# Twelve of the 192 expert-weight units loaded in three transfers (112, 8 and 8 rows) instead of one

## The reference

```python
def moe_swiglu(h, w_router, w_gate, w_up, w_down):
    logits = jnp.einsum('td,de->te', xt, w_router, preferred_element_type=jnp.float32)
    top_logit, top_idx = lax.top_k(logits, TOP_K)
    gates = jax.nn.softmax(top_logit, axis=-1)
    ...
        a = xb @ w_gate[e]
        b = xb @ w_up[e]
        y = (jax.nn.silu(a) * b) @ w_down[e]
        return y * gate[:, None].astype(y.dtype)
```

## Time and profile before

| | |
|---|---|
| median of 3 runs | 1385.05 us |
| lowest and highest run | 1382.86 and 1386.51 us |
| the profiled execution, its own time | 1383.68 us |
| its span, first to last instruction | 1381.9 us |
| TensorE busy | 1293.9 us, 94% of the span |
| VectorE, ScalarE, GpSimd busy | 421.2, 278.1, 103.7 us |
| bytes moved by DMA | 443.42 MB |
| largest chain shares | TensorE 83%, DMA 7%, VectorE 5% |

### The profile page before, as it was taken

The page is one execution under the profiler, slowest core; times in us unless marked ns, Lnnn a source line. Parts: engine busy times, 40 slices in busy tenths (PEclk is TensorE's granted clock), DMA queues, the critical chain, the costliest instruction groups (busy, mean ns, idle before and its releaser), DMA issues.

```text
span 1381.9 us, 30957 instructions
## 1 busy us (share of the span) xinstructions
PE 1293.9 (94%) x14359; PEld 803.1 (58%) x14359; DVE 421.2 (30%) x573; ACT 278.1 (20%) x409; POOL 103.7 (8%) x239
## 2 busy tenths in 40 slices
PE   5788999999989886999999999999989999999985
PEld 5776999999978874336344345346334345336333
DVE  5586644444455754011020031030021031031023
ACT  4355444433343533000000000000000000000001
POOL 3231400000000123700000000000000000000000
PEclk9999999999998999999999999999999999999998
DMA  9716755555554057999999999999999999999992
GB/s 312 241 62 215 218 186 185 188 188 187 186 195 148 34 228 320 379 406 389 408 426 424 426 424 424 426 425 425 425 425 426 425 427 422 428 423 424 421 416 97
DMA packets 63734, 443.42 MB, mean 321 GB/s; under 512 B 4440, under 2 KB 6496, under 8 KB 39024
## 3 DMA queue, kind: packets, MB, share of 16 engines
q1 hardware_dynamic: 61456, 433.46, 77.4%
q0 software_dynamic: 2144, 7.90, 2.0%
HBM read 440.30 MB, written 1.05 MB: 319 GB/s over the span
## 4 chain that ended last, share of the span: by engine, by line
PE 83%; DMA 7%; DVE 5%; ACT 1%; SPq 1%; issue 1%; POOL 0%; ACTq 0%; DVEq 0%
PE pd L923 17%; PE pa L914 13%; PE pb L914 13%; PE pc L914 9%; DMA unit<-in_moe_w_down 5%; PE pc L656 3%; PE pc L657 3%; PE pc L658 3%; PE pd L658 2%; PE pd L657 2%; PE pd L656 2%; DMA rwords_b<-in_na_rpb 2%; PE pa L656 2%; PE pa L658 2%; PE pa L657 2%; PE pa L868 2%
## 5 line engine op out<-in xcount | busy, mean ns | idle before, releaser
L923 PE MATMUL pd<-unit,hid 128*32 128x256 f32 x4704 | 260.2, 379 | 9.8 <-DMA unit<-in_moe_w_down 9.8
L914 PE MATMUL pa<-unit,xT 128*32 128x448 f32 x2048 | 240.2, 541 | 3.3 <-DMA unit<-in_moe_w_up 2.1
L914 PE MATMUL pb<-unit,xT 128*32 128x448 f32 x2048 | 240.3, 541 | 0.0
L923 PEld LDWEIGHTS pd<-unit,hid 128*32 128x32 f32 x4704 | 151.2, 110 | 116.4 <-DMA unit<-in_moe_w_down 11.9
L1196 DVE TENSOR_TENSOR w_lo<-ring,w_hi 128x2048 fp32r<-128x2048 f32 x72 | 170.7, 2372 | 139.6 <-ACT w_hi L1012 139.2
L1454 DVE TENSOR_TENSOR hidp<-hid,pa 128x448 f32<-128x448 f32 x16 | 14.8, 924 | 558.4 <-PE pa L914 558.4
L1012 ACT ACTIVATE w_hi<-ring 128x2048 fp32r<-128x2048 f32 x72 | 137.3, 1908 | 69.9 <-PE pb L658 56.4
L914 PE MATMUL pc<-unit,xT 128*32 128x448 f32 x1280 | 149.5, 539 | 0.0
L914 PEld LDWEIGHTS pa<-unit,xT 128*32 128x32 f32 x2048 | 66.3, 110 | 128.1 <-issue 120.4
L914 PEld LDWEIGHTS pb<-unit,xT 128*32 128x32 f32 x2048 | 66.6, 110 | 126.6 <-issue 126.6
L656 PE MATMUL pc<-hT_hi,w_hi 128*128 128x256 f32 x448 | 130.1, 290 | 5.4 <-DVE w_lo L1196 4.0
(11 more groups left out here) (261 smaller groups left out, 1321.9 us busy)
## 6 DMA issues: line engine op xcount, KB each, us to landing
unit<-in_moe_w_gate SPq DMA_DIRECT2D x64, 1792.0 KB, 27.7
unit<-in_moe_w_up SPq DMA_DIRECT2D x64, 1792.0 KB, 26.9
unit<-in_moe_w_down SPq DMA_DIRECT2D x64, 1792.0 KB, 28.8
ring<-in_dense_w_gate SPq DMA_DIRECT2D x8, 2048.0 KB, 8.9
ring<-in_dense_w_up SPq DMA_DIRECT2D x8, 2048.0 KB, 8.9
ring<-in_dense_w_down SPq DMA_DIRECT2D x8, 2048.0 KB, 7.6
ring<-in_w_in SPq DMA_DIRECT2D x7, 2048.0 KB, 7.9
ring<-in_w_out SPq DMA_DIRECT2D x4, 2048.0 KB, 11.7
```

What stands on the lines that cost most here:

```text
L914: ins = mm(bank(half, s)[quad(j)], xT[:, s, dt, :], w[:, at:at + FJ], start=dt == 0, stop=dt == DT - 1)
L923: ins = mm(down_out[s][quad(j)], e[:, half, s, t, :], w, start=half == t == 0 and s != 2, stop=half == 1 and t == FT - 1, skip_group_check ...
```

## The change

One unit in fourteen, from unit 24 on (the units 28, 42, 56, ... 182, twelve in all), is loaded by three transfers: rows 0 to 111, rows 112 to 119, rows 120 to 127. Each adds 16 to the buffer's semaphore, and the counts that TensorE waits for are raised to match. The loads of extra items are single, as before. It is described as loading "one unit in fourteen ... as 112 rows and twice eight rows, so that eight of the sixteen DMA engines carry nine rows of it and eight carry seven".

```diff
+SPLIT_EVERY = 14
+SPLIT_ROWS = (0, 112, 120, P)
...
+        def unit_rows(n):
+
+            return SPLIT_ROWS if n >= UNITS and n % SPLIT_EVERY == 0 else (0, P)
+
+        def loads_of_slot(slot, last):
+
+            return sum(len(unit_rows(n)) - 1 for n in range(slot, last + 1, SLOTS))
+
         def unit_loads(i, u):
             if isinstance(i, int):
-                return (i * UNITS + u) // SLOTS + 1
+                return loads_of_slot(unit_slot(i, u), i * UNITS + u)
             slot = u % EXTRA_SLOTS
-            return (i - NE) * EXTRA_TURNS + (-(-(NE * UNITS - slot) // SLOTS) + u // EXTRA_SLOTS + 1)
+            return (i - NE) * EXTRA_TURNS + (loads_of_slot(slot, NE * UNITS - 1) + u // EXTRA_SLOTS + 1)
...
                 slot = unit_slot(i, u)
-                sp.dma_start(units[slot][:, :], src).then_inc(unit_landed[slot], 16)
+                rows = unit_rows(i * UNITS + u) if isinstance(i, int) else (0, P)
+                for a, b in zip(rows, rows[1:]):
+                    sp.dma_start(units[slot][a:b, :], src[a:b]).then_inc(unit_landed[slot], 16)
```

## The result

| | before | after |
|---|---|---|
| median of the runs | 1383.95 us (4 runs) | 1538.61 us (4 runs) |
| lowest and highest | 1375.71 and 1386.51 | 1537.87 and 1539.76 |
| profiled execution, its span | 1383.68, 1381.9 | 1539.76, 1537.9 |
| TensorE busy | 1293.9 us | 1338.3 us |
| MB on the load queue | 433.46 | 433.47 |

A forecast was written before the change was run, and what follows sets the result against it. The prediction took unit 188's landing, set by the late half of the DMA engines, as the bound. A 5.9 us gain, all other terms 0, took 1385.05 to 1379.2 us; the range was 1377.0 to 1386.5.

The forecast's parts named there:

- What bounds the kernel: End of the kernel: the landing of unit 188, at 1347.1 us, sets the end; all after it is fixed.
- The cadence; about half the engines ahead: Units 42 to 188: 4.382 us each against 4.29, so about half the engines run up to 13.5 us ahead.
- Part 1: Eleven splits in the full queue: a row less on eight late engines lands unit 188 5.9 us earlier.
- rival A: Split units: the nine rows fall on the late eight engines, giving 1391.0 us, +0.43%; chance 0.16.
- Part 2: Other eight engines: 5.9 us more work, 1.7 us still in hand; cost 0, at worst a few tenths.
- Part 3: SP's queue: 24 more issues of 333 ns, 8.0 us in all, hidden by SP's waiting; price 0.
- Part 4: DMA engines: 24 more transfers, bounded by nothing or slight gain and 0.9 us; taken as 0.
- Part 5: TensorE's waits on units: larger counts cost 0; stalls shrink and the whole 5.9 us reaches the end.
- The tail of 34.8 us: After unit 188 lands: fixed work of TensorE, ScalarE and VectorE, 34.8 us, unchanged by the split.
- B: Split units: pieces don't tilt the load, or late engines don't match the split; 1385 us, 1382 to 1386; chance 0.12.
- C: Full queue: small transfers have a price; 0.27 us each cancels the gain, 0.13 leaves half, 1382; chance 0.04.
- the forecast: Whole kernel: the lighter eight engines are the late ones, giving 1379.2 us, range 1377.5 to 1381; chance 0.68.

The follow-up runs named there:

- base: The kernel before the change, run again unchanged as a control for profile and scatter: 1377.91 us, ratio 0.9987.
- more8: Kernel before the change, units whole, plus one load of eight rows of 1216 bytes into spare memory behind each unit from 24 on: 1388.52 us, ratio 1.007.
- cols3: Kernel before the change with the same twelve units cut into three transfers by columns, all 128 rows in each: 1380.91 us, ratio 1.0047.
- r112_16: The changed kernel with its twelve units split into two loads, 112 rows and 16 rows, so no tilt between engines: 1523.96 us.
- r8_far: The same twelve units each loaded as sixteen transfers of eight rows lying four partitions apart, all columns: 1511.55 us, 131.4 above the kernel before.
- one112: The change's split on one unit alone, unit 112, instead of twelve: 1393.26 us, ratio 1.01.
- run 12: Not a follow-up run: these words belong to "Half the engines run 12 us ahead", where run is a verb and 12 us the lead.

## Why the prediction was wrong, point by point

- *What bounds the kernel*: right. The landing of unit 188 still sets the end; it came 159.2 us later.
- *The cadence; about half the engines ahead*: right, by base's last stretch (share 0.51). The lead by then is 12 us long. That it is the same half all along is not shown, nor are the instruction blocks as its cause.
- *Part 1, a row less on eight engines, 11 x 0.536 = 5.9 us*: **here it failed, with part 4**. The step took 0.536 us a row, measured on loads of 128 rows only, for rows of a 112-row and an eight-row load too. In the slow stretches the share is 1.0 and the rate about half, so a row takes nearly twice as long: 424/230 x 0.536 = 0.99 us, and the packets there have 1.009. The step's condition, that the eight with seven rows are the late ones, was wrong as well: by more8 two of the late engines get nine rows. By that reading those two would have brought unit 188 later even with rows at full speed, as in rival A, and not 5.9 us earlier.
- *Part 2, a row more on the other eight, 1.7 us in hand*: wrong for two of the eight, which had nothing in hand. Its number, the lead, came back in the formula for the price of a split.
- *Part 3, SP's issues at nothing*: right, by cols3, which has as many loads (0.6 us by the trace).
- *Part 4, 24 transfers, 0 to 0.9 us*: the number of transfers is indeed cheap (cols3: 0.02 to 0.27 us each), but its bounds came from boundaries between *whole* loads. (Nor was the 432 GB/s row a faster one: at its share of 1.02 a busy engine moves 26.5 GB/s, against 26.2 in the long stretch.) The sentence said that no small transfer in the full queue existed before; the honest upper end was open, since nothing in the trace bounded the speed of a packet in another shape. The prediction rested on the cadence of full units, which says nothing about partial ones.
- *Part 5, waits 11.9 to 6.0 us*: wrong with part 1, 123.2 us.
- *The tail of 34.8 us*: 31.6 us in this run.
- *The rivals*: none priced slower packets. A and B moved work between engines at an unchanged speed. C had the right place and a price per small transfer of 0.27 us; r112_16 shows that the price is in the large piece as well. That GB/s falls with landings was named as a mark of C; it fell, but around the split units, not at them alone.
- *Whether nine rows fall on late or early engines (A against the forecast)*: on both, six early and two late. A and the forecast each took all eight for one kind, at chances of 0.16 and 0.68; B named late engines that don't match the split, but priced them at no loss. A unit lands with its last engine, so two late ones are enough for A's direction. How much of the 154.7 us this tilt makes is not shown: r112_16, without it, is 148.5 above its before, and a single run doesn't tell 6 us.

## What to carry to other kernels

A load into SBUF that spans all 128 partitions is more than the sum of its rows: on this chip one unit cut by rows, at unchanged bytes, cost 15 us (8 to 20) where its whole work is 4.3, and slowed whole units in the queue beside it; twelve units cut by columns cost 0.6 to 6.5 us together. So if a transfer must be divided, divide its columns and keep the partitions. In a profile, look at the DMA share and GB/s together: full share with a falling rate was slower packets here (share 1.01, 230 GB/s, 1.009 us a row against 0.541), and no counting of rows or bytes finds it. The mean share also hides which engine is last: a landing waits for the slowest of sixteen, and two late ones were enough. And a duration may be carried over to a new shape only with a bound that comes from some row of that shape.

## What the hardware showed that was not expected

- Packet speed changes with the partitions of a load: 26.2 GB/s for a busy engine in whole loads, 20.8 to 22.8 in the stretch with eight-row loads four partitions apart, 12.1 to 13.6 with neighbouring ones. With sixteen rows the order of the times is the other one: 147.5 us above before for neighbours, 179.1 for rows eight apart.
- An eight-row load runs on eight engines (1344 more packets in r8_far, eight for each load less the whole loads' sixteen); in more8 and in the changed kernel two of them belong to the late half.
- The damage of one split lasts 24 us where the engines are 7 us apart, 34 us late in the run.
- Half the engines run 12 us ahead of the other half at the end of the kernel before; one split doesn't close that: one112 still ends with half of them, 10 us long.

```profile
1354.00:1364.00 10.00, 10.00 (x180) 6.59 (x173) 3.00 (x6) 0.60 (x1) 0.00 (x0) 1.00 0.49 207
```

- An issue on SP is not always 333 ns. Seven issues in the last item of the kernel after:

```profile
L451 SPq DMA_DIRECT2D unit<-in_moe_w_down x7: 332/1684/4650, 1440.5 to 1475.2; - x7
...
DMA to landing us min/median/max: 43.6/45.9/52.9
```

Here an issue takes up to 4.65 us; what holds it back is not shown. It cost nothing visible, since landings came 43.6 us or more after it.
